# A smaller pool of weight buffers, with a place of its own for the low part, in a two-block fp32 network

## The reference

```python
def hybrid_layer(x, mem, ...):
    h = rms_norm(x, norm_pre)
    proj = h @ w_in                      # 1024 x (21 * 512 + 8, and 5 * 1024 gates)
    ...                                  # five branches: stick breaking, mLSTM, gating, retention, memory
    up = jnp.einsum('bsnw,nwd->bsnd', ys, w_up)
    merged = jnp.sum(jax.nn.sigmoid(gates.reshape(b_, s_, N_BRANCH, D_MODEL)) * up, axis=2)
    out = merged @ w_out
    return x + rms_norm(out, norm_post)

def mixer_ab(x, norm, w_in, conv_w, ...):
    z = rms_norm_2(x, norm) @ w_in
    xr = causal_dwconv(z_rec, conv_w, conv_b)
    y_a = jax.nn.gelu(z_gate) * rg_lru(xr, w_gx, b_gx, w_ga, b_ga, lam)
    ...
    return jnp.concatenate([y_a, y_b], axis=-1) @ w_out
```

## Time and profile before

| | |
|---|---|
| median of 3 runs | 1944.13 us (1941.7 to 1945.12) |
| profiled run | 1944.13 us |
| its span | 1942.0 us, 2.1 us less |
| mean granted clock of PE | 0.956 |
| PE busy | 1777.7 us (92%) |
| DVE busy | 1229.3 us (63%), of it low parts 673.8 us |
| ACT busy | 1024.0 us (53%), of it high parts 582.9 us |

### The profile page before, as it was taken

One profiled execution on the slowest core, in us unless ns is written; L12 is line 12 of the kernel. 1 busy time (PEld: TensorE's weight loads), 2 busy tenths in 40 slices (PEclk: granted clock), 3 DMA queues, 4 the chain that ended last, 5 costly groups with the idle time before them and its releaser, 6 DMA issues. The chain is left out here.

```text
span 1942.0 us, 26513 instructions
## 1 busy us (share of the span) xinstructions
PE 1777.7 (92%) x10479; PEld 1578.7 (81%) x10479; DVE 1229.3 (63%) x1661; ACT 1024.0 (53%) x1389; POOL 32.1 (2%) x58
## 2 busy tenths in 40 slices
PE   6999999999999999999999899999999218989998
PEld 6888888887888888888789788899989106879997
DVE  4755766666656567655767755566565995556664
ACT  5855556454667455645465755555455105545544
POOL 4000000000000000000000000000000000000000
PEclk9989999999999999999999999999999658999999
DMA  7535555565564555556555453566655103346663
GB/s 251 152 117 167 173 158 163 173 187 181 170 178 116 171 168 158 156 178 188 169 177 179 152 175 109 155 188 187 186 184 174 44 0 109 115 131 186 186 186 119
DMA packets 161914, 306.73 MB, mean 158 GB/s; under 512 B 12322, under 2 KB 16324, under 8 KB 161664
## 3 DMA queue, kind: packets, MB, share of 16 engines
q1 hardware_dynamic: 158928, 298.91, 50.7%
q0 software_dynamic: 2864, 6.14, 1.0%
HBM read 303.97 MB, written 1.05 MB: 157 GB/s over the span
## 5 line engine op out<-in xcount | busy, mean ns | idle before, releaser
L913 DVE TENSOR_TENSOR weights_lo<-weights_raw,weights_hi 128x1024 fp32r<-128x1024 f32 x562 | 673.8, 1223 | 522.1 <-ACT weights_hi L483 519.3
L483 ACT ACTIVATE weights_hi<-weights_raw 128x1024 fp32r<-128x1024 f32 x562 | 582.9, 1055 | 540.3 <-DMA weights_raw<-in_w_in_dram 196.0
L1465 PE MATMUL bank<-h_hi,weights_hi 128*128 128x256 f32 x1504 | 431.3, 287 | 27.4 <-DVE h_lo L950 13.4
L1465 PE MATMUL bank<-h_hi,weights_lo 128*128 128x256 f32 x1504 | 429.4, 286 | 0.0
L1465 PE MATMUL bank<-h_lo,weights_hi 128*128 128x256 f32 x1504 | 429.3, 285 | 0.0
L1447 PE MATMUL bank<-weights_hi,h_hi 128*128 128x512 f32 x928 | 368.9, 398 | 16.9 <-DVE h_lo L963 10.4
L1447 PE MATMUL bank<-weights_lo,h_hi 128*128 128x512 f32 x928 | 365.2, 394 | 0.0
L1447 PE MATMUL bank<-weights_hi,h_lo 128*128 128x512 f32 x928 | 364.7, 393 | 0.0
L1465 PEld LDWEIGHTS bank<-h_hi,weights_hi 128*128 128x128 f32 x1504 | 292.8, 195 | 30.0 <-DVE h_lo L950 14.8
L1465 PEld LDWEIGHTS bank<-h_hi,weights_lo 128*128 128x128 f32 x1504 | 292.7, 195 | 0.4
L1465 PEld LDWEIGHTS bank<-h_lo,weights_hi 128*128 128x128 f32 x1504 | 292.6, 195 | 0.0
(11 more groups left out here) (286 smaller groups left out, 1496.1 us busy)
## 6 DMA issues: line engine op xcount, KB each, us to landing
weights_raw<-in_w_in_dram SPq DMA_DIRECT2D x224, 512.0 KB, 3.6
weights_raw<-in_f_w_up_dram SPq DMA_DIRECT2D x96, 512.0 KB, 3.9
weights_raw<-in_f_w_down_dram SPq DMA_DIRECT2D x48, 512.0 KB, 3.6
weights_raw<-in_w_up_dram SPq DMA_DIRECT2D x40, 512.0 KB, 3.6
weights_raw<-in_c_w_pw_dram SPq DMA_DIRECT2D x24, 512.0 KB, 3.6
weights_raw<-in_ab_w_in_dram SPq DMA_DIRECT2D x20, 512.0 KB, 3.7
weights_raw<-in_w_mem_kv_dram SPq DMA_DIRECT2D x16, 512.0 KB, 3.6
weights_raw<-in_w_out_dram SPq DMA_DIRECT2D x16, 512.0 KB, 3.6
```

What stands on the lines that cost most here:

```text
L483: nc.scalar.activation(w_hi[:, q % SPLIT, 0:w], raw[:, n % RAW, 0:w], ACT.Copy).then_inc(hi_done, 1)
L913: tt(w_lo[:, n % RAW, 0:w], raw[:, n % RAW, 0:w], w_hi[:, q % SPLIT, 0:w].bitcast(F32), ALU.subtract)\
L1465: ins = mm(bs[i][:, j, :], wp[:, kk, f * P:(f + 1) * P], sp_[:, 2 * u + kk, :], start=first and u == us[0] and kk == 0 and n == 0 and j == ...
```

## The change

The raw buffer has five slots and no longer shares them with the low parts. The high and the low part have four slots each, both numbered by the place among the split units: 5 + 4 + 4 = 13 slots, the same memory. Since the raw slot is free once the low part is made, SP waits for lo_done of unit n - 5 (for the five unsplit units, still for PE). ACT's wait becomes PE's use of the split unit q - 4, by the same line as before with the new SPLIT. The bound in for_tile is now u + RAW - 1 with RAW = 5, so u + 4 in place of u + 5, with the condition on the unit SPLIT places back now four back. AHEAD is not used by anything.

```diff
--- before.py
+++ after.py
@@ -18,8 +18,9 @@
 H, HD = 4, P
 EPS = 1e-6
 BIG = 1e30
-RAW = 7
-SPLIT = 6
+RAW = 5
+SPLIT = 4
+AHEAD = 3
 BANKS = 8
 FF = 3 * D
 KF = FF // P
@@ -123,10 +124,9 @@
         h_hi = sb("h_hi", [P, KD, S], F32R)
         h_lo = sb("h_lo", [P, KD, S], F32R)
         memT = sb("mem_features", [P, KD, S])
-        with nc.sbuf_tensor("weights_lo", [P, RAW, 1024], F32R) as low_of_raw:
-            w_lo = low_of_raw
         raw = sb("weights_raw", [P, RAW, 1024])
         w_hi = sb("weights_hi", [P, SPLIT, 1024], F32R)
+        w_lo = sb("weights_lo", [P, SPLIT, 1024], F32R)
         with nc.sbuf_tensor("arena_parts", [P, 24, 1024], F32R) as parts_of_arena:
             arr = parts_of_arena
         arena = sb("arena", [P, 24, 1024])
@@ -356,7 +356,7 @@
 
             def for_tile(name, i, stage=None):
                 n, u = PC.split_at((name, i), stage), PC.unit_at((name, i), stage)
-                while 0 < n < len(SPLITS) and SPLITS[n] < u + RAW - 2 and (n < SPLIT or SPLITS[n - SPLIT] < u - 1):
+                while 0 < n < len(SPLITS) and SPLITS[n] < u + RAW - 1 and (n < SPLIT or SPLITS[n - SPLIT] < u - 1):
                     n += 1
                 up_to(n)
 
@@ -376,7 +376,9 @@
                 r = n % RAW
                 if n == RAW:
                     sp.dma_start(cst[:, P:C_ALL], A["constants"][:, P:C_ALL]).then_inc(const_in, 16)
-                if n >= RAW:
+                if n >= RAW and n - RAW in NTH:
+                    sp.wait_ge(lo_done, NTH[n - RAW] + 1)
+                elif n >= RAW:
                     sp.wait_ge(pe_done, PC.at(n - RAW, "unit"))
                 k, m = src.shape[1], src.shape[2]
                 dst = raw[:, r, 0:k * m].rearrange("p (k m) -> p k m", k=k)
@@ -910,7 +912,7 @@
 
                 dve.wait_ge(hi_done, q + 1)
                 w = width(n)
-                tt(w_lo[:, n % RAW, 0:w], raw[:, n % RAW, 0:w], w_hi[:, q % SPLIT, 0:w].bitcast(F32), ALU.subtract)\
+                tt(w_lo[:, q % SPLIT, 0:w], raw[:, n % RAW, 0:w], w_hi[:, q % SPLIT, 0:w].bitcast(F32), ALU.subtract)\
                     .then_inc(lo_done, 1)
 
             up_to, for_tile, past = splitter(VC, emit)
@@ -1424,7 +1426,7 @@
                 q = NTH[n]
                 PC.split += 1
                 pe.wait_ge(lo_done, q + 1)
-                return [x[:, i, 0:k * m].rearrange(shape, k=k) for x, i in ((w_hi, q % SPLIT), (w_lo, n % RAW))]
+                return [x[:, q % SPLIT, 0:k * m].rearrange(shape, k=k) for x in (w_hi, w_lo)]
 
             def used(ins, *names):
 
```

## The result

The changed kernel takes 1997.4 us (1994.7 to 1999.4, 4 runs) against 1943.3 us before (1941.7 to 1945.1, 4 runs): 1.0276 times as long, 95% interval 1.0261 to 1.0293. That is 54.1 us more; the forecast was 1996 us. Its profiled run took 1998.1 us, with a span of 1995.9 us and a mean granted clock of 0.950 (0.956 before).

A forecast was written before the change was run, and what follows sets the result against it. PE (TensorE) bounds the kernel, busy 1777.7 of 1942.0 us. 1944.1 + 44.0 (layer 0 14.4, layer 1 9.3, AB 11.3, boundaries 7.2, C and FFN 1.8) + 8 for clock = 1996 us; range 1980 to 2012, eight in ten 1963 to 2018.

The forecast's parts named there:

- The supply of weights runs ahead of PE in undisturbed stretches: Away from blocks of other work, low parts are ready about 6 us early; 540-odd of 562 units priced at 0.
- the leads: F0 and F1 after each gelu: low parts 0.4 to 1.0 us early at 11 places, just missed at two, +1.2.
- the rival in which FFN tips over: The 11 FFN places are each missed by 1 to 1.5 us: +15 and +10 for clock, 2021 us; chance 0.13.
- The subtraction at each block: Block end plus one low part, minus PE's arrival: layer 0 14.4, layer 1 9.3, AB 11.3 us.
- the term of 4.7 for unit 327: Stage AB: late copy of unit 325 moves sigmoid, tanh and exp by 1.9 us; low part 327 comes late, +4.7.
- The boundaries: L0 to L1, L1 to AB, X1 to F1: +2.4 us each, sum 7.2; the other boundaries 0.
- The clock: PE runs slow after gaps: 0.8 us each for seven new gaps and three longer boundaries, about 8 in all.
- the table load behind unit 12: Layer 0 gate block: about 1.0 of 5.1 us comes back, as an ACT table load no longer follows a late copy.
- The rival of absorbed stalls: Early PE stalls pull later DVE and ACT work out of its way: +22 to +25, 1969 us; chance 0.15.
- the norm of F1: At X1 to F1 a low part before the norm waits for a high part that waits for PE: 2.4 us later.

The follow-up runs named there:

- experiment 1: Kernel before with its slots and waits, only the changed kernel's look-ahead rule, so parts stand in the changed kernel's places: 1990.4 us, ratio 1.0239.
- experiment 2: Kernel before with its buffers, the changed kernel's look-ahead rule in stage AB alone: 1954.0 us, ratio 1.0053.
- experiment 3: Look-ahead bound one unit further, once in the changed kernel (2013.5 us) and once in the kernel before (2019.1 us).
- experiment 5: Changed kernel with three raw slots: 2053.1 us with four high, four low and same order; 2036.1 us with five, five and look-ahead one unit further.
- experiment 6: Changed kernel, but SP waits for PE's use of unit n-5 instead of its low part before refilling a raw slot: 2013.4 us, ratio 1.0361.
- experiment 4: Kernel before with its buffers, look-ahead one unit shorter: 1945.5 us, ratio 1.0012.

## Why the prediction was right

The supply of weights runs ahead of PE in undisturbed stretches: right. X0 moved by 0.0 and F0 by -0.4 us. In F0 and F1 PE waits for a low part once each, as often as I had said, for 0.24 us where I had 0.6 each; the leads held at all the other places, and the rival in which FFN tips over fell with them. PE's row in F0, the one in F1 reads the same at 1804.78:

```profile
1304.39 0.39 PE L1467 MATMUL bank<-h_hi,weights_hi 128*128 128x256 f32 x1 [0.24 <-DVE weights_lo L915]
```

The subtraction at each block: right in mechanism, shown by experiment 1, and close in size. Predicted against measured gap: unit 12 5.1 and 5.15; unit 20 3.5 and 3.58; unit 121 3.35 and 3.44; unit 334 (5.4 above what stood there: 7.0) and 7.04; unit 78 2.8 and 1.91. In L1 the six are within 0.2 us of the forecast. In AB the term of 4.7 for unit 327 came in two pieces: the late sigmoid also held a bank for which PE waits at unit 323, which made the way there 1.3 us longer, and the gap at 327 added 3.3 (9.48 less the 6.13 that stood at 328), together 4.6. I had the whole of it at 327. PE's row at unit 323, with the sigmoid as the releaser:

```profile
1097.86 0.36 PE L1467 MATMUL bank<-h_hi,weights_hi 128*128 128x256 f32 x1 [1.09 <-ACT arena L773]
```

The boundaries: 2.4 us each predicted; measured 3.75 - 1.83 = 1.92 at L0 to L1, the same at L1 to AB, and 5.72 - 4.18 = 1.54 at X1 to F1. At the first two this is luck: the working was wrong. I had two more low parts right before the low parts of x on DVE. DVE's timeline there, before and after, shows four of them (units 155 to 158) and then three (154 to 156):

```profile
508.04 3.12 DVE L1215 SCALAR_TENSOR_TENSOR x_tokens<-arena,statistics,x_tokens 128x512 f32<-128x512 f32 x4
...
515.24 3.50 DVE L913 TENSOR_TENSOR weights_lo<-weights_raw,weights_hi 128x1024 fp32r<-128x1024 f32 x3 [0.34 <-ACT weights_hi L483]
518.91 1.23 DVE L913 TENSOR_TENSOR weights_lo<-weights_raw,weights_hi 128x1024 fp32r<-128x1024 f32 x1 [0.18 <-ACT weights_hi L483]
```

```profile
527.60 1.23 DVE L915 TENSOR_TENSOR weights_lo<-weights_raw,weights_hi 128x1024 fp32r<-128x1024 f32 x1 [2.77 <-ACT weights_hi L485]
528.75 3.10 DVE L1217 SCALAR_TENSOR_TENSOR x_tokens<-arena,statistics,x_tokens 128x512 f32<-128x512 f32 x4
...
535.94 3.50 DVE L915 TENSOR_TENSOR weights_lo<-weights_raw,weights_hi 128x1024 fp32r<-128x1024 f32 x3 [0.34 <-ACT weights_hi L485]
```

The low part at 527.60 is that of unit 153. It now stands ahead of the last step of the residual (L1217, L1215 before) and waits 2.77 us for its high part, which ACT makes only behind a table load. The residual starts 5.7 us behind PE's start of unit 150 (at 523.06) where it was 2.1 us before (at 505.94): 3.6 us later, and 1.4 us of it come back because one low part fewer follows. The result, 2.2 us, is near the 2.4 of the forecast by chance.

The clock: mis-sized, 8 us taken, about 11 measured. Windows of one unit each behind the new gaps (stretch, sum, busy, granted clock, DMA share, GB/s):

```profile
64.85:70.40 5.55, 5.55 (x13) 0.50 0.78 230
99.82:104.10 4.28, 4.28 (x25) 0.68 0.74 218
296.96:299.90 2.94, 2.94 (x13) 1.00 0.64 196
432.52:437.10 4.58, 4.58 (x13) 0.64 0.66 221
1147.31:1152.80 5.49, 5.49 (x13) 0.51 0.76 245
```

The windows run into the next unit's first matmul (x13 and x25 are 12 and 24 matmuls and one more). From one unit's start to the next one's it is 5.29 us at unit 12 for 2.73 at clock 0.50 (the lower level, 1.2 GHz, all along), 4.11 at unit 20 for 2.88, 4.39 at unit 121, 5.29 at unit 334, and 2.80 at full clock behind the short gap at unit 78. With what the unit behind still lost, the price is 2.8 + 1.6 + 0.1 + 1.7 + 2.6, and again 0.1 and 1.7 in L1 (units 228 and 283), 10.6 in all. I had capped it at 1.5 us a gap because I had one row to read (0.67 behind 6.13 us); the cap was wrong, gaps of 3.4 us already cost 1.7. Of the boundaries, which I had at 0.8 each, only X1 to F1 cost clock, 1.1 us. The sum came out since the three boundaries, units 78 and 228, and FFN were too dear, by 0.4 to 1.5 us each. The Trainium skill, "TensorE: Matmul & The Clock Gate", Part 1, has the ramp penalty at under 1% of a typical kernel span. Taken over all of the span, this trace doesn't agree: PE was busy for 75.3 us of the span before in stretches at the lower level, and for 100.2 us after; if nearly half of that is loss, as at unit 12, this is an estimate of 36 and 48 us, 1.9% and 2.4% of the span. The new part alone, about 11 us, is 0.6% of the span and a fifth of the whole loss.

The rival of absorbed stalls had its cases: about 1 us at the table load behind unit 12 as I had it, and some 3.6 us in the memory tiles behind unit 20, where the stage ends no later for it. They offset the larger clock term in L0, and the second may be in part the spread (2.2 us in the run of experiment 1). As a whole the rival fell, by experiment 2 and by the sum.

What I had seen at one place only, the norm of F1, is the other side of the place. Elsewhere I treated a part as something that can only be too late. Experiments 3, 5 and 6 show that its waits are inherited by whatever stands behind it, and the first two boundaries of the changed kernel show it too. The forecast could do without this in nearly all of its terms, because the change moved parts later; for a change that moved them earlier the same working would have given the wrong sign, as my own expectations for experiment 3 did.

## What to carry to other kernels

When a buffer pool shrinks, look at how its size sets the order of instructions as well as at slots: for each block of other work, subtract when PE comes to the first unit that isn't ready from when the block ends, and add the slow clock behind the gaps that are left, nothing to 2.8 us each here. An engine in order has two ways to lose at such a place, the part behind the block or the block behind a part that waits, so the look-ahead is a number to be tried in both directions, anew for each number of slots, and best set place by place: what ran at 1945.5 us with seven and six slots took 2013.5 with five, four and four. Before a measured difference is put down to the order or to the buffers, change each at the other's old and new value; here the buffers were worth 7 or 68 us. Freeing a slot one step earlier was worth 16 us.

## What the runs showed of the hardware that I had not expected

A gap of PE of 3.44 or 3.58 us was followed by a unit at 0.64 or 0.68 of the clock and cost 1.6 to 1.7 us more, one of 1.91 us next to nothing. The length of the gap doesn't set the price. Behind 5.15 and 7.04 us the unit ran at 0.50 and 0.51, behind 9.48 us it took 4.20 us for 2.88, less than double. Behind the boundary of 3.75 us it took 4.31, behind 1.83 us at the same place before 4.44. A gap of 2.54 us, at unit 13 in experiment 4, cost 1.7 us (unit 13 took 4.42 us for 2.73), and the one of 2.52 us at 79.30 before nothing. And the gap of 3.58 us at unit 20 cost 1.6 us in the changed kernel and 0.1 us in the run with the order alone, where the same unit ran at full clock. PE's row and the window there, to be held against 99.82 above:

```profile
99.55 0.38 PE L1465 MATMUL bank<-h_hi,weights_hi 128*128 128x256 f32 x1 [3.58 <-DVE weights_lo L913]
...
99.55:103.83 4.28, 4.28 (x35) 1.00 0.05 7
```

So the clock price of a gap of one length at one place differed by 1.5 us between two runs, and part of the spread of the stage times may be this.
